# Differential-attention scores on rounded operands in three products, with one maximum instruction for both components

## The reference, cut to what matters

```python
def block(i):
    start = i * Q_BLOCK
    qb = lax.dynamic_slice_in_dim(q, start, Q_BLOCK, axis=3)
    s = jnp.einsum('bhcqd,bhckd->bhcqk', qb, k, preferred_element_type=jnp.float32) * scale
    causal = (start + jnp.arange(Q_BLOCK))[:, None] >= key_pos[None, :]
    s = jnp.where(causal, s, -jnp.inf)
    p = jax.nn.softmax(s, axis=-1)
    attn = p[:, :, 0] - lam * p[:, :, 1]
    return jnp.einsum('bhqk,bhkv->bhqv', attn.astype(v.dtype), v)
```

## Time and profile before

| what | us |
|---|---|
| median of 3 executions | 1469.87 (1469.55 to 1470.52) |
| the profiled execution | 1469.3 |
| its span, first to last instruction | 1467.6 |
| PE busy | 1433.6 (98%) |
| DVE busy | 951.9 (65%) |
| ACT busy | 664.2 (45%) |
| POOL busy | 90.7 (6%) |
| granted TensorE clock | 0.997 of full speed |
| attention, from its first score to the first `mk` product | 333.10 to 444.56 |

### The profile page before, as it was taken

The page is one execution under the profiler, slowest core; times in us unless marked ns, Lnnn a source line. Parts: engine busy times, 40 slices in busy tenths (PEclk is TensorE's granted clock), DMA queues, the critical chain, the costliest instruction groups (busy, mean ns, idle before and its releaser), DMA issues. The chain is left out here.

```text
span 1467.6 us, 19675 instructions
## 1 busy us (share of the span) xinstructions
PE 1433.6 (98%) x7272; PEld 1190.8 (81%) x7280; DVE 951.9 (65%) x1559; ACT 664.2 (45%) x1298; POOL 90.7 (6%) x132
## 2 busy tenths in 40 slices
PE   9999999999989999999999989999999999999998
PEld 7889888885669988888887878888888788888886
DVE  4883565628878524543553798887776576467898
ACT  6324222327776424433432665444455464444443
POOL 1000000000002001010000360000000000000011
PEclk9999999999999999999999999999999999999999
DMA  9212111102003611311231333664343797766463
GB/s 318 60 30 58 29 30 29 57 2 87 1 1 124 243 58 73 107 59 43 72 109 50 134 117 115 215 200 172 145 158 120 236 348 265 261 222 193 156 229 129
DMA packets 94606, 185.52 MB, mean 126 GB/s; under 512 B 10160, under 2 KB 28592, under 8 KB 92464
## 3 DMA queue, kind: packets, MB, share of 16 engines
q1 hardware_dynamic: 87312, 153.30, 31.0%
q10 hardware_dynamic: 7200, 30.97, 6.2%
HBM read 142.30 MB, written 41.94 MB: 126 GB/s over the span
## 5 line engine op out<-in xcount | busy, mean ns | idle before, releaser
L2179 PE MATMUL ps<-wh,oph 128*128 128x512 f32 (+1 forms) x576 | 216.0, 375 | 0.0
L2181 PE MATMUL ps<-wh,opl 128*128 128x512 f32 (+1 forms) x576 | 212.1, 368 | 0.0
L2180 PE MATMUL ps<-wl,oph 128*128 128x512 f32 (+1 forms) x576 | 211.9, 368 | 0.0
L2179 PE MATMUL ps<-d_ring 128*128 128x512 f32 x448 | 174.6, 390 | 2.1 <-DVE d_ring L2053 2.1
L2181 PE MATMUL ps<-d_ring 128*128 128x512 f32 x448 | 174.5, 390 | 0.0
L2180 PE MATMUL ps<-d_ring 128*128 128x512 f32 x448 | 174.3, 389 | 0.0
L775 POOL TENSOR_TENSOR rms<-stat,mhalf 128x1 f32<-128x1 f32 (+2 forms) x59 | 54.4, 924 | 1326.9 <-DVE stat L1388 1305.2
L2181 PEld LDWEIGHTS ps<-wh,opl 128*128 128x128 f32 x576 | 108.3, 188 | 19.2
L2180 PEld LDWEIGHTS ps<-wl,oph 128*128 128x128 f32 x576 | 108.4, 188 | 17.7
L2179 PEld LDWEIGHTS ps<-wh,oph 128*128 128x128 f32 x576 | 108.3, 188 | 17.7 <-ACT vt L968 0.2
L1306 ACT ACTIVATE d_ring<-left_raw 128x512 fp32r<-128x512 f32 x112 | 70.4, 629 | 96.6 <-PE ps L2181 74.2
(11 more groups left out here) (362 smaller groups left out, 2928.8 us busy)
## 6 DMA issues: line engine op xcount, KB each, us to landing
right_raw<-in_w_down_dram SPq DMA_DIRECT2D x128, 256.0 KB, 3.9
u_kept_s<-us SPq DMA_DIRECT2D x64, 256.0 KB, 2.2
left_raw<-u_kept_s SPq DMA_DIRECT2D x64, 256.0 KB, 2.8
w_blk<-in_w_up_blocks_dram ACTq DMA_DIRECT2D x14, 1024.0 KB, 5.6
left_raw<-u_kept_a SPq DMA_DIRECT2D x48, 256.0 KB, 3.0
raw<-in_w_in_dram SPq DMA_DIRECT2D x16, 512.0 KB, 3.9
u_kept_a<-u SPq DMA_DIRECT2D x24, 256.0 KB, 2.3
x_in<-in_x_dram SPq DMA_DIRECT2D x8, 512.0 KB, 9.2
```

Of the source, the lines that this page charges most:

```text
L2179: te.matmul(o, lh, rh, start=first, stop=False)
L2180: te.matmul(o, lh, rl, start=False, stop=False)
L2181: return te.matmul(o, ll, rh, start=False, stop=last)
```

## The change

The change has four parts. ACT copies `kt` and `qt` block by block to `k_hi` and `q_hi` with rounding to float32r, two blocks on each of the steps n = 52 to 59, all keys first and then the queries in the order in which they are used. DVE subtracts them from the originals in the same steps and writes the rests in place of the originals (`k_lo`, `q_lo`). `scores` makes three float32r products for each component where there was one float32 product, and waits at each new block of queries for its rest. `attn_max` makes one reduction over both components, which waits for both and stands ahead of the combination of the step before. `q_hi` lies where B and C of the scan lay, `k_hi` in scratch space, and a junk tile of ACT's squares moves to make room.

```diff
+QK_TILES = [("k", i) for i in range(NT)] + [("q", i) for i in MIX_TILES]
+QK_FIRST = 52
...
+        q_hi, q_lo = at("q_hi", "X", 16384, [P, DH, T], F32R), at("q_lo", "Q", 0, [P, DH, T], F32R)
+        k_hi, k_lo = at("k_hi", "TMP", 0, [P, DH, T], F32R), at("k_lo", "K", 0, [P, DH, T], F32R)
+        y_junk = at("y_junk", "MISC", 0, [P, DH, P])
...
+            def query_key_hi(x):
+
+                name, i = QK_TILES[x]
+                if x == 0:
+                    act.wait_ge(rt_ev, 2 * NT)
+                    act.wait_ge(ssd_b, NT)
+                    act.wait_ge(ssd_y, NT)
+                src, dst = (qt, q_hi) if name == "q" else (kt, k_hi)
+                s.activation(dst[:, :, i * P:(i + 1) * P], src[:, :, i * P:(i + 1) * P], ACT.Copy).then_inc(qk_hi, 1)
...
+                if 0 <= n - QK_FIRST < NT:
+                    query_key_hi(2 * (n - QK_FIRST))
+                    query_key_hi(2 * (n - QK_FIRST) + 1)
...
-                act.wait_ge(mx_done[c], n + 1)
+                act.wait_ge(mx_done, n + 1)
...
+            def query_key_lo(x):
+
+                name, i = QK_TILES[x]
+                dve.wait_ge(qk_hi, x + 1)
+                raw_qk, hi, lo = (qt, q_hi, q_lo) if name == "q" else (kt, k_hi, k_lo)
+                cols = slice(i * P, (i + 1) * P)
+                v.tensor_tensor(lo[:, :, cols], raw_qk[:, :, cols], hi[:, :, cols].bitcast(F32), ALU.subtract).then_inc(qk_lo, 1)
...
-            def attn_max(n, c):
-                keys = (steps[n][0] + 1) * P
-                dve.wait_ge(s_done[c], n + 1)
+            def attn_max(n):
+                i = steps[n][0]
+                dve.wait_ge(s_done, 2 * n + 2)
                 if n >= 2:
-                    dve.wait_ge(ex_done[c], n - 1)
-                b = score_bank(steps[n][0], c)
-                src = ps[:, b:b + 2, :].rearrange("p b k -> p (b k)")
-                v.tensor_reduce(nmax[:, n % 2, c:c + 1], src[:, 0:keys], AX.X, ALU.max, negate=True).then_inc(mx_done[c], 1)
+                    dve.wait_ge(ex_done[0], n - 1)
+                    dve.wait_ge(ex_done[1], n - 1)
+                b, nb = score_bank(i, 0), 2 if i >= 4 else 1
+                src = ps[:, b:b + 2 * nb, :].rearrange("p (c b) k -> p c (b k)", c=2)
+                v.tensor_reduce(nmax[:, n % 2, :], src[:, :, 0:(i + 1) * P], AX.X, ALU.max, negate=True).then_inc(mx_done, 1)
...
             for n in range(NS + 3):
                 if n < NS:
-                    attn_max(n, 0)
+                    attn_max(n)
                 if 1 <= n <= NS:
                     attn_comb(n - 1)
-                if n < NS:
-                    attn_max(n, 1)
...
             def scores(n):
                 i, h = steps[n]
+                if h == 0:
+                    pe.wait_ge(qk_lo, NT + MIX_TILES.index(i) + 1)
...
-                    for c in range(2):
-                        half = slice(64 * c, 64 * c + 64)
-                        te.matmul(ps[:, score_bank(i, c) + k0 // 512, 0:kn], qt[half, h, i * P:(i + 1) * P], kt[half, h, k0:k0 + kn],
-                                  start=True, stop=not diag)
+                    for part, (q, k) in enumerate(((q_hi, k_hi), (q_hi, k_lo), (q_lo, k_hi))):
+                        for c in range(2):
+                            half = slice(64 * c, 64 * c + 64)
+                            te.matmul(ps[:, score_bank(i, c) + k0 // 512, 0:kn], q[half, h, i * P:(i + 1) * P], k[half, h, k0:k0 + kn],
+                                      start=part == 0, stop=part == 2 and not diag)
```

More of the change, by code:

```diff
@@ L439, in build @@
         gate_done, lam_s = sem("gate_done"), sem("lam_s")
-        s_done = [sem(f"s_done{c}") for c in range(2)]
-        mx_done = [sem(f"mx_done{c}") for c in range(2)]
+        s_done, mx_done = sem("s_done"), sem("mx_done")
         ex_done = [sem(f"ex_done{c}") for c in range(2)]
         comb_done, pt_done, pt_ev, pv_done, o_ev = (sem(n) for n in ("comb_done", "pt_done", "pt_ev", "pv_done", "o_ev"))
-        o_sq = sem("o_sq")
+        o_sq, qk_hi, qk_lo = sem("o_sq"), sem("qk_hi"), sem("qk_lo")
         resid_loaded = sem("resid_loaded")
@@ L991, in _ @@
                     act.wait_ge(gate_done, i + 1)
-                    square(("y", i), mix[:, 0:4, i * P:(i + 1) * P], junk[:, 0:512].rearrange("p (k c) -> p k c", k=4))
+                    square(("y", i), mix[:, 0:4, i * P:(i + 1) * P], y_junk[:])
             steps = ATT_STEPS
@@ L1640, in _ @@
                     ssd_last(SSD_LAST[n])
+                if 0 <= n - QK_FIRST < NT:
+                    query_key_lo(2 * (n - QK_FIRST))
+                    query_key_lo(2 * (n - QK_FIRST) + 1)
                 if n >= Y_DONE + 2:
@@ L2377, in scores @@
                     diag = k0 + kn == (i + 1) * P
-                    for c in range(2):
-                        half = slice(64 * c, 64 * c + 64)
-                        te.matmul(ps[:, score_bank(i, c) + k0 // 512, 0:kn], qt[half, h, i * P:(i + 1) * P], kt[half, h, k0:k0 + kn],
-                                  start=True, stop=not diag)
+                    for part, (q, k) in enumerate(((q_hi, k_hi), (q_hi, k_lo), (q_lo, k_hi))):
[3 more added lines that the diff above has]
+                                      start=part == 0, stop=part == 2 and not diag)
                 for c in range(2):
                     kn = (i + 1) * P - (i // 4) * 512
-                    te.matmul(ps[:, score_bank(i, c) + i // 4, kn - P:kn], ident_b[:], mask_q[:], start=False, stop=True).then_inc(s_done[c], 1)
+                    te.matmul(ps[:, score_bank(i, c) + i // 4, kn - P:kn], ident_b[:], mask_q[:], start=False, stop=True).then_inc(s_done, 1)
             def mem_tile(i):
```

## The result

| | before | after |
|---|---|---|
| median of 22 runs each, us | 1468.77 (1467.36 to 1471.09) | 1471.36 (1468.63 to 1474.11) |
| ratio, with its 95% interval | | 1.0015 (1.0008 to 1.0021) |
| profiled execution, its span | 1469.3, 1467.6 | 1468.7, 1467.0 |
| attention, first score to first `mk` product | 111.46 | 112.62 |

The changed kernel is slower by 2.2 us by the ratio (0.0015 of 1469; the two medians lie 2.6 apart), less than the 2.9 us that the forecast took as the least it could tell from no change, though 22 runs a side put the whole interval above 1. The 1471.36 lie 0.4 above the forecast of 1471.0. That is closer than the reasoning deserves: the kernel before measured 1.1 us less here than in the three runs that the forecast stood on, and the change cost 2.2 us instead of 1.1. That two errors of opposite sign nearly cancelled is luck.

A forecast was written before the change was run, and what follows sets the result against it. In the attention a ring of dependent engine steps sets the pace of smaller blocks, PE that of (7, 3). A longer ring adds 1.0 us and step 9 0.1, rounding nothing: 1469.3 to 1470.4, plus 0.57 gives 1471.0; range 1467.5 to 1475.0.

The forecast's parts named there:

- part 1: Attention scores: three float32r products replace one float32 product, 4.3 us less PE work if component pairs stay side by side.
- Rival 1: Scores: the pairs of float32r products run one after the other, about +18 us, 1489 us; chance 0.12.
- rival 2: Scores: a 128-column float32r product takes 0.21 us instead of 0.12, +1.4 us more, 1472.4; chance 0.20.
- The ring: Attention: large scores, merged reduction, small step's combination, its transposes, then next scores; pairs 0.18, 0.20, 0.16 and 0.10 us longer.
- part 2: DVE maxima: one reduction saves 0.15 us a step but stands whole ahead of the previous step's combination, lengthening the ring.
- Rival 3: Merged reduction does not hold the small step's T0 up; some 3 us gained, 1467.2 at the lowest; chance 0.11.
- The sum over the stretch: Whole attention: start delay, longer pairs and step 9, less idle time taken up, total +1.1 us.
- the stall at T1 of step 6: PE's 1.00 us wait for ACT there absorbs the 0.9 us delay accumulated by step 8, leaving zero.
- The clock: PE clock stays at 2.4 GHz, since no gap of PE grows over what it had.

The follow-up runs named there:

- e3: Changed kernel with float32 scores and no rounding, keeping one merged reduction in every step; 1473.61 us, ratio 1.0036 to the kernel before.
- e2: Changed kernel with three float32r products, but two split reductions in all steps, in their old places around the combination; 1469.53 us, ratio 1.0005.
- e4: Changed kernel with the merged reduction in the small steps only and two reductions in the large steps; 1464.55 us, ratio 0.9971.
- e8: Changed kernel with the merged reduction in the large steps only and two reductions in the small steps; 1472.35 us, ratio 1.0026.
- e7: Kernel before with the merged reduction in the small steps only, float32 scores and no rounding; 1467.45 us, ratio 0.9991.
- e10: Repeat of e4: three products, merged reduction in the small steps only; 1465.00 us, ratio 0.9975.
- e9: Changed kernel with two unused PE products ahead of the wait for the combination in each small step; 1470.18 us, ratio 1.0008.
- e12: Repeat of e9, the changed kernel with two unused products filling PE's wait; 1470.29 us, ratio 1.0011.
- e5: Kernel before with the 16 rounding copies and 16 subtractions added, results unused, float32 scores, split reductions; 1469.20 us, ratio 1.0004.
- e1: The changed kernel, unaltered, run again against the kernel before; 1470.93 us, ratio 1.0014.
- e11: The changed kernel, unaltered, run a third time beside e12; 1470.50 us, ratio 1.0011.
- e6: Changed kernel with the loops over component and part exchanged, so one component's three products are issued together; 1471.30 us, ratio 1.0018.

## Why the prediction was right, and where it was not

**The products** (part 1). Pairs of records stood side by side, as taken, and their starts 0.23 us apart at 512 columns, 0.17 to 0.18 at 384 (0.53 for three was taken), 0.12 at 256. Rival 1 is out. At 128 columns the timeline of a step of block 4 reads:

```profile
428.15 0.22 PE L2410 MATMUL ps<-k_hi,q_hi 64*128 64x128 f32 x2
428.21 0.27 PE L2410 MATMUL ps<-k_lo,q_hi 64*128 64x128 f32 x2
428.32 0.28 PE L2410 MATMUL ps<-k_hi,q_lo 64*128 64x128 f32 x2
```

They follow each other by 0.06 and 0.11; over all steps the median is 0.11. The 0.12 of the sum was too much, and (4, 0) gains 0.10 where 0.02 was booked (e3 against after): rival 2, the likeliest of the three at 0.20, is out on the other side. Over all steps PE's work from score to mask fell by 5.1 us where 4.3 was forecast, and the mis-sized blocks of 128 make up most of the difference. The Trainium skill's figure for a load of 128 columns (TensorE: Matmul & The Clock Gate, LDWEIGHTS), columns by 1.2 or 0.107 us, lies near this distance of 0.11. By it the pairs of (4, 0) would have been 5.16 us apart, nearer the measured 5.15 than the 5.20 of the forecast. The records of the loads themselves last longer here, 0.18 to 0.19 us each.

**The ring** (part 2). Measured 7.74, 6.85, 5.95 and 5.15 against 7.69, 6.82, 5.92 and 5.20. The reductions took, in groups by form:

```profile
L1686 DVE TENSOR_REDUCE nmax<-ps 128x2 f32<-128x2048 f32 x4 | 9.2, 2288 | 3.2 <-PE ps L2414 3.2
...
L1686 DVE TENSOR_REDUCE nmax<-ps 128x2 f32<-128x1280 f32 x4 | 6.0, 1490 | 1.8 <-PE ps L2414 1.8
```

The two between took 2.02 and 1.76 us. The line through the earlier trace rows gave 2.29, 2.03, 1.76 and 1.49. Rival 3, in which the merged reduction holds nothing up, fails by this and by e2, e3, e4 and e8: the 0.5 a pair in (7, 3) that it promised does not show even in e2, where nothing is merged.

**The sum over the stretch.** From the first score to that of step 8: 30.07 us against 29.15, 0.92 late for the forecast 0.9. There the stall at T1 of step 6 took it up, as said, and PE's timeline now has

```profile
366.31 0.63 PE L2429 MATMUL ps<-ident,probs 128*128 128x128 f32 x4 [0.29 <-ACT probs_t L1042]
```

for the 1.00 us of the earlier trace rows. At step 12 the two kernels stand at 378.66 and 378.64, 0.2 late from their own starts (0.1 forecast); from there to the end it is 66.87 against 65.92, or 0.95 for the forecast 1.0. The stretch is 1.16 longer, and 1.1 was the forecast.

**The clock.** The step that failed is the sentence "The clock stays at 2.4 GHz: no gap of PE grows over what it had". The waits at T0(B), of which the earlier trace rows had none and which the forecast itself foresaw, are such gaps, and the wait ahead of the scores of step 2 grew from 0.66 to 1.50 us. The gap at T0 of step 9, the changed kernel's longest in the attention, against the half clock in its last part or in the 1.2 us behind it:

| kernel | gap, us | half clock there, from |
|---|---|---|
| e7 | 0.72 | no |
| before | 1.19 | no |
| e4; e10; e3; e9 and e12 | 1.23; 1.24; 1.25; 1.26 | no |
| e5; e2 | 1.51; 1.62 | no |
| after; e1; e11; e6 | 1.92; 1.92; 1.93; 1.91 | no; 376.30; 377.46; 379.28 |
| e8 | 2.56 | 378.68 |

With float32 scores the merge left the gap as it was (e3), split maxima with the short scores made it 1.62 (e2), and both together 1.92. But e5, with float32 scores and split maxima like the kernel before, has 1.51, so some 0.3 of this can be other than the scores and the merge. On DVE the normalisation of the memory tokens stands first, then the maximum of step 10, and behind it the combination for which T0 of step 9 waits. In the profile of before and in that of after:

```profile
374.30 1.08 DVE L1657 TENSOR_REDUCE nmax<-ps 128x1 f32<-128x896 f32 x1
```

```profile
373.57 2.02 DVE L1686 TENSOR_REDUCE nmax<-ps 128x2 f32<-128x1792 f32 x1
...
375.94 0.62 DVE L1696 SCALAR_TENSOR_TENSOR probs<-probs,ratio 128x384 f32<-128x384 f32 x1
```

The maximum is 0.94 us longer. Counted from the first score of the attention, T0 starts 0.4 us later than before, and PE, with its scores shorter, comes 0.3 earlier: together the 0.7 by which the gap grew. The forecast booked 0.1 us for this, as a delay, and did not look at it as idle time of PE; it had seen that PE's saving becomes waits, and not that this one would be added to a gap of 1.19. The clock accounts for 0.7 to 1.0 us of the 2.2, and for a part of the spread of the single runs, 1468.6 to 1474.1 against 1467.4 to 1471.1.

What is shown and what is not: that half clock comes more often in the changed kernel than in the one before is shown, by 15 of 45 runs against 10 of 87 at 0.995 or less. That filling the waits at T0(B) undoes it rests on 1 of 22 runs and is less firm: side by side, e12 had 1 of 11 and e11 2 of 11, and only e9 with 0 of 11 against 5 of 10 of e6 stands clearly apart. That it is the gap at step 9 is what the table points to, 4 of 5 profiles from 1.91 us on and none of 9 below, and it is not shown: the filling shortened some ten waits at once, and e2, with 1.62 there and split maxima, has a mean clock of 0.9959 like the changed kernel. Pieces also stand at other places. That of e6 at 345.15 is behind a wait of 0.60 us, and those at 444.13 (e6) and 443.75 (e3) are behind waits of 1.14 and 0.56, where the kernel before waits 1.43 and 0.56. Why one execution gets it and the next does not, the traces do not tell.

**A trap in the two profiles.** The profiled execution of after is 0.6 us faster than that of before, though its attention is 1.16 slower. At 848 us it is still 0.8 late. There PE waits 2.05 us in both, first before, then after:

```profile
847.61 0.50 PE L2179 MATMUL ps<-oph,wq_h 128*128 128x512 f32 x1 [2.05 <-DVE wq_l L1925]
```

```profile
848.40 0.50 PE L2206 MATMUL ps<-oph,wq_h 128*128 128x512 f32 x1 [2.05 <-DVE wq_l L1952]
```

Behind this wait the changed kernel ran at half clock from 849.11 on, the one before did not, and at 860 us the changed one is 2.4 late. At 880 us the kernel before waits 3.18 us, where the changed one waits 1.80, and then has half clock from 880.51 on; from 890 us on the changed one is 0.5 to 0.6 ahead. Another piece of before, at 703.02 behind a wait of 2.09 us, was made up by 740 us. None of these comes from the change: the third profile of the changed kernel (e11) has both places of before, at 705.14 and 882.63. Two single executions cannot settle a matter of 1 us here; only the stretch does, and the runs for the total.

## What to carry to other kernels

Where one instruction on an in-order engine replaces two, ask what stood between them. Here the same merge is worth 1.7 us or more in the small steps, where the work between was long and its customer late, and costs the ring in the large ones, where PE was waiting for the short work in between; chosen by kind of step, it makes the kernel 0.9971 of before. And a saving of 5.1 us on an engine that is busy at 97% may be worth 0.5 (e2) until what really sets the pace is out of the way, and then 2.3 us (e10 against e7). Last, a lengthened wait of PE may cost more than its own length: look at the granted clock behind it over several executions, not one.

## What the runs showed of the hardware that was not expected

- Three float32r products of a component issued one behind the other, and then three of the other component, ran as two streams side by side on the two halves of the rows, their records 10 ns apart: the order of issue between the halves was not the order of starts (e6).
- Float32r products of 64 rows follow each other by 0.23 us at 512 columns, 0.12 at 256 and still 0.11 at 128: halving the columns once more gains hardly anything. That the loads of weights set this limit was not tested.
- Busy work on PE with one wait of 1.9 to 2.6 us in it was followed in four of five profiles (e1, e11, e6, e8) by 3.41 us at 1.2 GHz, at a cost of some 1.5 us, in the fifth (after) by none. One and the same wait of 2.05 us, near 848 us, was followed by it in after and not in before.
